# The RG-LRU gates computed per block of 88 instead of per tile of 128, in five groups between the xr and yr products

## The chip, the cores and the metric

One core of one Trainium2 chip runs the whole program. The metric is the device time of one execution in microseconds. The kernel before takes 2645.93 us, the median of three runs (2645.75 to 2646.18).

## What is computed

Two layers of a streaming encoder trunk on x of shape 1 x 512 x 1024, float32. Each layer is half a SwiGLU feed-forward, a mixing block, and another half feed-forward. The change lies in the mixing block's branch A:

```python
def block_diag_linear(x, w, b):                       # 16 blocks of 88 channels
    xb = x.reshape(B, S, RNN_BLOCKS, RNN_BLOCK_DIM)
    return jnp.einsum('bshi,hij->bshj', xb, w).reshape(B, S, D_RNN) + b

def rg_lru(x, w_a, b_a, w_x, b_x, lam):               # D_RNN = 1408 = 16 * 88 = 11 * 128
    r = jax.nn.sigmoid(block_diag_linear(x, w_a, b_a))
    i = jax.nn.sigmoid(block_diag_linear(x, w_x, b_x))
    log_a = -LRU_C * r * jax.nn.softplus(-lam)
    inp = jnp.sqrt(-jnp.expm1(2.0 * log_a)) * (i * x)
    # h[s] = exp(log_a[s]) * h[s-1] + inp[s], a scan over the 512 positions
    ...

xr, yr, q, k, v, g_a, g_b = split(h @ w_in)
u = causal_depthwise_conv(xr)                         # width 4
y_a = (gelu(yr) * rg_lru(u)) @ w_up_a
y_b = chunked_attention(q, k, v) @ w_up_b
x = x + (sigmoid(g_a) * y_a + sigmoid(g_b) * y_b) @ w_out
```

## The kernel before

Everything is held feature-major: a tile is 128 features by 512 positions, and a product leaves one tile in one PSUM bank. Each float32 value is split into a high part and a low remainder, and each product (`product`, L1237 to L1244) is three matmuls: high weight with low activation, high with high, low weight with high activation.

**The ring.** Weights come in chunks of up to 128 x 1024. Each goes through four steps: SP loads it into `raw` (`load`, L341 to L347), ACT copies its high part (`ring`, L511), POOL subtracts to make the low part (L470), and PE uses it. There are four slots. ACT may convert a chunk once PE has begun the third chunk before it; SP may load one once POOL has made the low part of the fourth before it. Each engine's order is written out by hand, so a wait on one engine also delays everything written behind it there. SP has only the loads and the band loads of the attention in its queue.

**Order of the mixing block on PE.** The eleven xr tiles (five `pair` calls of two chunks each and one `single`), then the recurrence gates, then the eleven yr tiles, the eight g_a tiles, w_up_a, q and k, the attention, w_up_b, w_out. One pair is 48 matmuls.

**xr and u.** DVE scales an xr tile out of its bank into `tmp` (L992), which frees the bank. ACT starts the convolution (`conv_init`, L642), DVE adds three taps (`conv`, L1000, `tmp` and `u` in SBUF), ACT takes u's high part (`conv_hi`, L648) and DVE its low part (L839). Two tiles are handled at a time.

**The gates.** The two 1408 x 1408 matrices are block-diagonal with blocks of 88, and the tiles are of 128, so each output tile draws on up to three input tiles. `rg_blocks` lists 52 blocks of weights per layer; 42 are used whole and 10 hold two half-height parts, used by two matmuls on different rows of the array: 186 matmuls (L1389). All come after the last xr product. ACT turns each bank into a gate by a sigmoid (L519), DVE multiplies u by the input gate (L1027). Then ACT runs tanh (L682), and the chain of logarithms and exponentials (L692 to L700) alternates with DVE's subtraction, product and scan (L1041 to L1049). DVE's `yr_out`, which frees the yr banks, stands between its scans. Last come gelu (L712) and the split of the result (`ya_hi`, L524; `ya_lo`, L839), with ring steps of ACT between them.

**Banks.** The products from xr on use six banks in turn (`mix_bank`).

**The attention.** For each of eight pairs of heads, PE turns ten blocks of the probabilities per head by transposes in three groups (`turn`, L1493), with the first two of eight steps of a g_b product between them, computes the next pair's scores (L1435), the other six steps, and the weighted sum (L1508):

```python
turn(0)
gate_b([0])
turn(1)
gate_b([1])
turn(2)
if t + 1 < KD:
    scores(t + 1, (*LATE, 0, 1))
gate_b([2, 3, 4, 5, 6, 7])
weighted(t)
```

All three groups go through the same two banks, 4 and 5.

## Time and profile before

| | us |
|---|---|
| median of three runs | 2645.93 |
| the profiled execution's own time | 2646.78 |
| its span in the trace | 2644.6 |
| PE busy, share of the span | 2636.7, 100% |
| ACT, POOL, DVE busy | 1117.8, 1142.4, 909.0 |
| DMA, share of 16 engines by the queue of SP | 31.8% |

The profile was taken in an execution of its own, 0.85 us above the median of the runs; its span leaves out 2.2 us around the first and last instruction. Matmuls are pipelined: one row lasts 0.39 us although the next starts 0.227 us behind it, so time on PE is read from the starts of successive rows, and not from the durations.

### The profile page before, as it was taken

The page shows a single profiled execution, that of the slowest core. Times are in us where ns is not written, and L with a number is a line of the kernel's source. Part 1 is how long each engine was busy: PE and PEld are TensorE (multiplying, and loading weights), DVE is VectorE, ACT ScalarE, POOL GpSimd, SP SyncE. Part 2 cuts the span into 40 slices and gives each one's busy share as a digit, 9 for nine tenths or more (in the row PEclk, how much of TensorE's full clock was granted, in tenths as well). Part 3 has the DMA queues.
Part 4 walks back from the last instruction along what each step waited for, and adds up shares of the span by engine and source line. Part 5 has one row for each costly group of instructions (what it writes and reads, how often), then busy time and mean ns, then how long its engine had stood idle before and what let it go on. Part 6 is the DMA issues. An engine that isn't in the chain of part 4 may idle for free.

```text
span 2644.6 us, 32094 instructions
## 1 busy us (share of the span) xinstructions
PE 2636.7 (100%) x11988; PEld 2141.2 (81%) x11988; DVE 909.0 (34%) x1585; ACT 1117.8 (42%) x1621; POOL 1142.4 (43%) x484
## 2 busy tenths in 40 slices
PE   9999999999999999999999999999999999999999
PEld 7888887888876788888888888878888768888887
DVE  4223137651345332221132231567313453322210
ACT  5333235742546443332243332457435464433321
POOL 4444444445431344444444444444553313444443
PEclk9999999999999999999999999999999999999999
DMA  5333633333322323332333333332333232333322
GB/s 160 96 95 100 223 92 87 98 93 110 91 72 88 97 81 110 95 95 96 97 103 95 95 93 98 95 92 81 102 106 99 64 105 88 90 101 95 95 92 76
DMA packets 255233, 260.64 MB, mean 99 GB/s; under 512 B 9056, under 2 KB 241536, under 8 KB 255136
## 3 DMA queue, kind: packets, MB, share of 16 engines
q1 hardware_dynamic: 250640, 250.71, 31.8%
q10 hardware_dynamic: 4496, 8.57, 1.0%
q8 instruction: 68, 1.11, 0.2%
q14 instruction: 29, 0.24, 0.0%
HBM read 257.07 MB, written 10.57 MB: 101 GB/s over the span
## 4 chain that ended last, share of the span: by engine, by line
PE 97%; DVE 1%; ACT 1%; DMA 0%; issue 0%; SPq 0%; POOL 0%; DVEq 0%; ACTq 0%; POOLq 0%
PE ps L1239 29%; PE ps L1244 29%; PE ps L1243 29%; PE ps L1389 2%; PE ps L1493 1%; PE ps L1435 1%; PE ps L1508 1%; PE ps L1453 1%; PE ps L1458 1%; PE ps L1457 1%; DVE u L1000 1%; PE ps L1416 0%; PE ps L1415 0%; ACT p L779 0%; DMA raw<-in_w_in 0%
## 5 line engine op out<-in xcount | busy, mean ns | idle before, releaser
L470 POOL TENSOR_TENSOR wlo<-raw,whi 128x1024 fp32r<-128x1024 f32 x472 | 1141.0, 2421 | 1480.8 <-ACT whi L511 1480.8
L1239 PE MATMUL ps<-h_lo,whi 128*128 128x512 f32 x2272 | 889.2, 391 | 0.1
L1244 PE MATMUL ps<-h_hi,wlo 128*128 128x512 f32 x2272 | 884.5, 389 | 0.0
L1243 PE MATMUL ps<-h_hi,whi 128*128 128x512 f32 x2272 | 884.1, 389 | 0.0
L511 ACT ACTIVATE whi<-raw 128x1024 fp32r<-128x1024 f32 x472 | 495.2, 1053 | 708.9 <-PE ps L1239 670.2
L1239 PEld LDWEIGHTS ps<-h_lo,whi 128*128 128x128 f32 x2272 | 426.5, 188 | 93.2 <-issue 4.6
L1244 PEld LDWEIGHTS ps<-h_hi,wlo 128*128 128x128 f32 x2272 | 426.4, 188 | 89.3
L1243 PEld LDWEIGHTS ps<-h_hi,whi 128*128 128x128 f32 x2272 | 426.6, 188 | 86.5
L1239 PE MATMUL ps<-act_lo,whi 128*128 128x512 f32 x704 | 274.0, 389 | 0.0
L1244 PE MATMUL ps<-act_hi,wlo 128*128 128x512 f32 x704 | 273.9, 389 | 0.0
L1243 PE MATMUL ps<-act_hi,whi 128*128 128x512 f32 x704 | 273.9, 389 | 0.0
L889 DVE TENSOR_TENSOR tmp<-ps,square 128x512 f32<-128x512 f32 x88 | 60.9, 691 | 387.4 <-PE ps L1244 387.4
L524 ACT ACTIVATE act_hi<-tmp 128x512 f32 x88 | 55.0, 633 | 240.5 <-DVE tmp L894 240.5
L1244 PEld LDWEIGHTS ps<-act_hi,wlo 128*128 128x128 f32 x704 | 132.1, 188 | 27.7
L1243 PEld LDWEIGHTS ps<-act_hi,whi 128*128 128x128 f32 x704 | 132.1, 188 | 27.3
L1239 PEld LDWEIGHTS ps<-act_lo,whi 128*128 128x128 f32 x704 | 132.1, 188 | 27.2
L905 DVE SCALAR_TENSOR_TENSOR x<-ps,x 128x512 f32<-128x512 f32 x32 | 22.0, 688 | 384.2 <-PE ps L1244 384.2
L884 DVE TENSOR_TENSOR gate<-ps,square 128x512 f32<-128x512 f32 x88 | 60.5, 691 | 263.5 <-PE ps L1244 252.9
L573 ACT ACTIVATE gate<-gate 128x512 f32<-128x512 f32 x88 | 55.2, 631 | 110.1 <-DVE gate L884 110.0
L779 ACT ACTIVATE p<-p,mx 128x512 f32<-128x512 f32 (+3 forms) x128 | 70.1, 550 | 23.1 <-DVE mx L1137 23.1
L1000 DVE SCALAR_TENSOR_TENSOR u<-tmp,par,u 128x511 f32<-128x511 f32 (+2 forms) x66 | 75.4, 1155 | 4.3 <-ACT u L642 2.8
L894 DVE TENSOR_TENSOR tmp<-tmp,gate 128x512 f32<-128x512 f32 x88 | 70.2, 839 | 0.0
(173 smaller groups left out, 2656.3 us busy)
## 6 DMA issues: line engine op xcount, KB each, us to landing
raw<-in_w_in SPq DMA_DIRECT2D x124, 512.0 KB, 3.8
raw<-in_w_gate SPq DMA_DIRECT2D x88, 512.0 KB, 3.8
raw<-in_w_up SPq DMA_DIRECT2D x88, 512.0 KB, 3.8
raw<-in_w_down SPq DMA_DIRECT2D x80, 512.0 KB, 3.5
rel_band<-rel_rows ACTq DMA_DIRECT2D x1, 8192.0 KB, 41.8
raw<-in_w_up_b SPq DMA_DIRECT2D x16, 512.0 KB, 4.0
raw<-in_w_out SPq DMA_DIRECT2D x16, 512.0 KB, 3.5
raw<-in_rg_band SPq DMA_DIRECT2D x14, 448.0 KB, 3.4
```

Of the source, the lines that this page charges most:

```text
L470: nc.gpsimd.tensor_tensor(wlo[:, s, :], raw[:, s, :], whi[:, s, :].bitcast(F32), ALU.subtract).then_inc(lo_made, 1)
L511: nc.scalar.activation(whi[:, s, :], raw[:, s, :], ACT.Copy).then_inc(hi_made, C.made(hi_made))
L524: nc.scalar.activation(dst, src, ACT.Copy).then_inc(split_hi, C.made(split_hi))
L573: nc.scalar.activation(gate[:, m, :], gate[:, m, :], ACT.Silu).then_inc(silu_made, C.made(silu_made))
L779: nc.scalar.activation(part, part, ACT.Exp, scale=-1.0, bias=mx[:, e, i:i + 1], accum_out=total[:, e, i:i + 1]).then_inc(exp_made, C.made( ...
L884: nc.vector.tensor_tensor(gate[:, m, :], ps[:, m, :], rstd, ALU.mult).then_inc(bank_read[m], C.made(bank_read[m]))
L889: nc.vector.tensor_tensor(tmp[:, m, :], ps[:, 2 + m, :], rstd, ALU.mult).then_inc(bank_read[2 + m], C.made(bank_read[2 + m]))
L894: nc.vector.tensor_tensor(tmp[:, m, :], tmp[:, m, :], gate[:, m, :], ALU.mult).then_inc(to_split, C.made(to_split))
L1000: ins = nc.vector.scalar_tensor_tensor(u[:, t, back:S], tmp[:, t % 2, 0:S - back], col("conv_w", (CONV - 1 - back) * KR + t), u[:, t, back ...
L1239: ins = pe.matmul(ps[:, b, :], w_hi, x_lo, start=start, stop=False)
L1243: pe.matmul(ps[:, b, :], w_hi, x_hi, start=False, stop=False)
L1244: return pe.matmul(ps[:, b, :], w_lo, x_hi, start=False, stop=stop)
```

## The change

The gates are computed per block of 88. One block is six matmuls of 88 rows and 88 columns, 96 per layer. For that u's two parts must lie block by block from partition 0, and the gates must come back tile by tile. Both ways go by DMA from SBUF to SBUF, issued by SP, between its loads. A block crosses a tile's edge or not, so it is one or two pieces: 26 pieces for 16 blocks. Each piece is one DMA for u (both parts), one for the gate r and one for the gate i. Three buffers take blocks of u, two take blocks of gates.

The order on PE becomes: xr tiles 0 to 5, blocks 0 to 2, xr 6 and 7, blocks 3 to 5, xr 8 and 9, blocks 6 to 8, xr 10, blocks 9 and 10, yr 0 and 1, blocks 11 to 15, yr 2 to 10. The gates' weights are five chunks in place of eight. The xr tile is now scaled in its bank and stays there until the convolution has read it.

```diff
+NB = RNN // RB
+GROUPS = [(0, 3), (3, 6), (6, 9), (9, 11), (11, 16)]
+HELD = 3
@@ SP
+            def u_moves(l, b):
+                sp.wait_ge(u_split, l * KR + pieces(b)[-1][0] + 1)
+                if b >= HELD:
+                    sp.wait_ge(for_act, KD + l * 2 * NB + 2 * (b - HELD + 1))
+                for m, p0_, p1_, to in pieces(b):
+                    sp.dma_start(block_u[b % HELD][to:to + p1_ - p0_, :, :].bitcast(F32),
+                                 u_parts[p0_:p1_, :, m, :].bitcast(F32)).then_inc(u_moved[b % HELD], 16)
+            def gates_move(l, b):
+                sp.wait_ge(gate_made, l * 2 * NB + 2 * b + 1)
+                for m, p0_, p1_, to in pieces(b):
+                    sp.dma_start(r[p0_:p1_, m, :], block_gates[b % 2][to:to + p1_ - p0_, 0, :]
+                                 ).then_inc(gates_moved[b % 2], 16)
+                sp.wait_ge(gate_made, l * 2 * NB + 2 * b + 2)
+                for m, p0_, p1_, to in pieces(b):
+                    if m >= HELD:
+                        sp.wait_ge(gated, l * KR + m - HELD + 1)
+                    sp.dma_start(i_gate[p0_:p1_, m % HELD, :], block_gates[b % 2][to:to + p1_ - p0_, 1, :]
+                                 ).then_inc(gates_moved[b % 2], 16)
...
+                half_pair(YR0, 3, 1)
+                gates_move(l, 11)
+                u_moves(l, 14)
+                gates_move(l, 12)
+                u_moves(l, 15)
+                gates_move(l, 13)
+                half_pair(YR0, 4, 0)
+                gates_move(l, 14)
+                gates_move(l, 15)
+                half_pair(YR0, 4, 1)
@@ ACT
+                def gates(first, last):
+                    for b in range(first, last):
+                        if l or b >= 2:
+                            act.wait_ge(gates_moved[b % 2], moved(l, b, 2, 2) - 32 * len(pieces(b)))
+                        for g in range(2):
+                            act.wait_ge(for_act, C.next(for_act))
+                            nc.scalar.activation(block_gates[b % 2][0:RB, g, :], ps[0:RB, BANK["gate", 2 * b + g], :],
+                                                 ACT.Sigmoid, bias=col("b_x" if g else "b_a", b)[0:RB, :]
+                                                 ).then_inc(gate_made, C.made(gate_made))
...
+                decayed(6, 7)
+                ring()
+                gates(11, NB)
+                ring()
+                decayed(7, KR)
@@ DVE
+                def xr_out(b):
+                    dve.wait_ge(for_dve, C.next(for_dve))
+                    nc.vector.tensor_tensor(ps[:, b, :], ps[:, b, :], rstd_mix[:, :], ALU.mult
+                                            ).then_inc(xr_scaled, C.made(xr_scaled))
@@ DVE, conv
-                            u[:, t, back:S], tmp[:, t % 2, 0:S - back], col("conv_w", (CONV - 1 - back) * KR + t),
+                            u[:, t, back:S], ps[:, b, 0:S - back], col("conv_w", (CONV - 1 - back) * KR + t),
@@ DVE
+                u_made(8, 9)
+                u_gated(4, 5)
+                u_made(10)
+                u_gated(6)
+                yr_out(0)
+                yr_out(1)
+                u_gated(7, 8, 9, 10)
@@ PE
+                def gates(first, last):
+                    s = chunk()
+                    for b in range(first, last):
+                        pe.wait_ge(u_moved[b % HELD], moved(l, b, HELD, 1))
+                        for g in range(2):
+                            to, at = BANK["gate", 2 * b + g], (2 * (b - first) + g) * RB
+                            bank_free(to)
...
@@ PE, attention
                     turn(0)
-                    gate_b([0])
                     turn(1)
-                    gate_b([1])
                     turn(2)
                     if t + 1 < KD:
-                        scores(t + 1, (*LATE, 0, 1))
-                    gate_b([2, 3, 4, 5, 6, 7])
+                        scores(t + 1, (2, 0, 3, 1))
+                    gate_b(list(range(KD)))
                     weighted(t)
```

`moved` gives the count that a semaphore has once a block's pieces have landed. `bank_free` waits for the bank's last reader, for a gate's bank also for its sigmoid. With banks given out in PE's new order, the last two gates of each of the first three groups fall on the banks of the two xr tiles just before them (`BANK`). In the attention, the second group of transposes goes through banks 1 and 3 (`TURN_BANK`), the others stay in 4 and 5. The sigmoid's table of ACT is loaded ahead of the first convolution, and tanh is spread between the groups (`decayed`). `yr_out` of tiles 0 and 1 comes ahead of the scans, the others move back accordingly. The loops of POOL over the ring are written anew, with the same instruction per chunk. The gates' biases are laid out per block, ten columns more in `par`.

## Rows read from the trace of the kernel before

**Rows 1.** The page: its heading, busy time, the chain by engine.
```profile
span 2644.6 us, 32094 instructions
PE 2636.7 (100%) x11988; PEld 2141.2 (81%) x11988; DVE 909.0 (34%) x1585; ACT 1117.8 (42%) x1621; POOL 1142.4 (43%) x484
PE 97%; DVE 1%; ACT 1%; DMA 0%; issue 0%; SPq 0%; POOL 0%; DVEq 0%; ACTq 0%; POOLq 0%
```

**Rows 2.** Timeline of PE, gates of layer 0: start, length, engine, line, operation.
```profile
433.29 0.39 PE L1389 MATMUL ps<-u_lo,whi 128*128 128x512 f32 x1
...
444.57 0.47 PE L1389 MATMUL ps<-u_lo,whi 128*128 128x512 f32 x1 [0.73 <-ACT r L519]
...
473.96 0.39 PE L1239 MATMUL ps<-h_lo,whi 128*128 128x512 f32 x1
...
478.72 0.39 PE L1239 MATMUL ps<-h_lo,whi 128*128 128x512 f32 x1
```

**Rows 3.** Timeline of PE, first gate and first yr matmul of layer 1.
```profile
1745.33 0.39 PE L1389 MATMUL ps<-u_lo,whi 128*128 128x512 f32 x1
...
1786.02 0.39 PE L1239 MATMUL ps<-h_lo,whi 128*128 128x512 f32 x1
```

**Rows 4.** Timeline of DVE: second tile scaled, then the six taps of xr 4 and 5.
```profile
406.29 0.69 DVE L992 TENSOR_TENSOR tmp<-ps,rstd_mix 128x512 f32<-128x512 f32 x1 [0.20 <-PE ps L1244]
406.98 7.58 DVE L1000 SCALAR_TENSOR_TENSOR u<-tmp,par,u 128x511 f32<-128x511 f32 x6
```

**Rows 5.** Two lines of DVE over the run: shortest, median, longest in ns.
```profile
L1000 DVE SCALAR_TENSOR_TENSOR u<-tmp,par,u x66: 737/750/2896, 386.9 to 1752.1; 128x511 f32<-128x511 f32 x22, 128x510 f32<-128x510 f32 x22, 128x509 f32<-128x509 f32 x22
...
L905 DVE SCALAR_TENSOR_TENSOR x<-ps,x x32: 679/691/692, 281.5 to 2640.2; 128x512 f32<-128x512 f32 x32
```

**Rows 6.** Timeline of POOL beside those taps.
```profile
408.87 2.92 POOL L470 TENSOR_TENSOR wlo<-raw,whi 128x1024 fp32r<-128x1024 f32 x1 [0.67 <-ACT whi L511]
```

**Rows 7.** Timeline of ACT: a sigmoid, a ring step, first logarithm, first ya_hi.
```profile
444.32 0.68 ACT L519 ACTIVATE gate<-ps,par 128x512 f32<-128x512 f32 x1
444.89 1.06 ACT L511 ACTIVATE whi<-raw 128x1024 fp32r<-128x1024 f32 x1
...
485.01 0.63 ACT L697 ACTIVATE gate<-scan 128x512 f32<-128x512 f32 x1
...
533.75 0.63 ACT L524 ACTIVATE ya_hi<-tmp 128x512 fp32r<-128x512 f32 x1 [6.94 <-DVE tmp L1056]
```

**Rows 8.** SP's issues: back to back at L412 (ns), their landing; a weight load's landing.
```profile
L412 SPq DMA_DIRECT2D tmp<-rel_band x44: 444/597/599, 692.0 to 2165.7; - x44
...
DMA to landing us min/median/max: 2.3/2.7/4.7
...
raw<-in_w_in SPq DMA_DIRECT2D x124, 512.0 KB, 3.8
```

**Rows 9.** Stages: busy us per engine, granted clock, DMA share, GB/s.
```profile
0.00:5.00 5.00, 2.81 (x13) 2.81 (x14) 0.00 (x0) 1.28 (x1) 1.30 (x12) 1.00 0.53 166
5.00:10.00 5.00, 4.73 (x35) 4.33 (x34) 0.00 (x0) 1.34 (x2) 2.35 (x1) 1.00 1.01 322
400.00:480.00 80.00, 79.27 (x361) 60.24 (x360) 51.20 (x53) 45.20 (x61) 35.60 (x16) 1.00 0.33 93
```

**Rows 10.** Timeline of PE through one pair of heads.
```profile
791.38 1.09 PE L1493 MATMUL ps<-ident,p 128*128 128x128 f32 x8
792.23 0.47 PE L1239 MATMUL ps<-h_lo,whi 128*128 128x512 f32 x1
...
795.15 2.43 PE L1435 MATMUL ps<-k,q 64*128 64x512 f32 x16
797.51 0.50 PE L1239 MATMUL ps<-h_lo,whi 128*128 128x512 f32 x1
...
804.13 1.09 PE L1493 MATMUL ps<-ident,p 128*128 128x128 f32 x8
```

**Rows 11.** Timeline of ACT, the second copy out of the transposes' banks.
```profile
792.57 0.59 ACT L792 ACTIVATE square<-ps 128x512 f32<-128x512 f32 x1
```

More of the change, by code:

```diff
@@ L338, in _, with load @@
             place = [0]
-            def load(src, shape):
+            def load(src, shape, held=P):
                 s = place[0] % SLOTS
@@ new lines, in gate_weights, with half_pair, last_tile @@
+                def gate_weights(n):
+                    first, last = (2 * b * RB for b in GROUPS[n])
+                    load(bands[:, bass.ds(l, 1), first:last], (1, last - first), RB)
+                def half_pair(base, j, g):
+                    a, b = G8[g]
+                    load(win[:, bass.ds(l * KD + a, b - a), base + j * PAIR:base + (j + 1) * PAIR], (b - a, PAIR))
+                def last_tile(base):
+                    load(win[:, bass.ds(l * KD, KD), base + (KR - 1) * P:base + KR * P], (KD, P))
@@ L663, in _ @@
-                conv_init(KR - 1)
-                conv_hi(KR - 1)
-                chunks = 0
-                for m in range(KR):
-                    for g in range(2):
-                        while chunks * BPC <= rg_at(m, g)[-1]:
-                            ring()
-                            chunks += 1
-                        if g and m >= 2:
-                            act.wait_ge(gated, C.next(gated))
-                        read(mix_bank(RG_T + 2 * m + g), gate[:, m % 2, :] if g else r[:, m, :], ACT.Sigmoid,
-                             bias=col("b_x" if g else "b_a", m))
@@ new lines, in decayed @@
+                def decayed(first, last):
+                    for m in range(first, last):
+                        act.wait_ge(gated, C.next(gated))
+                        nc.scalar.activation(scan[:, m, :], r[:, m, :], ACT.Tanh, scale=decay[:, 0, m:m + 1]
+                                             ).then_inc(tanh_made, C.made(tanh_made))
+                sum_high()
+                ring(2)
+                rstd_from(0, rstd_mix[:, :])
+                act.preload_act_table_set("sigmoid_and_others")
@@ new lines, in _ @@
+                C.step(bank_read[1])
+                conv_init(0)
+                conv_init(1)
+                ring()
+                conv_hi(0)
+                conv_hi(1)
+                ring()
+                conv_init(2)
+                conv_init(3)
+                ring()
+                conv_hi(2)
+                conv_hi(3)
+                ring()
+                conv_init(4)
+                conv_init(5)
+                ring()
+                gates(0, 3)
+                conv_hi(4)
@@ L1016, in _, with yr_out, ga_out, u_made @@
+                def yr_out(t):
+                    scaled(y[:, t, :], BANK["yr", t])
+                def ga_out(t):
+                    scaled(ya_out[:, t, :], BANK["g", t])
+                def u_made(*tiles):
+                    for t in tiles:
+                        xr_out(BANK["xr", t])
+                    dve.wait_ge(xr_scaled, C.now(xr_scaled))
+                    if tiles[0] == 2:
                         dve.wait_ge(col_turned, C.next(col_turned))
                         nc.vector.tensor_copy(rstd_col[:, :], ps[:, 1, 0:S:P]).then_inc(bank_read[1], C.made(bank_read[1]))
-                    for n in both:
-                        conv(n)
@@ L1020, in _ @@
-                    for n in both:
-                        lo_of(u_lo[:, n, :], u[:, n, :], u_hi[:, n, :])
-                for m in range(KR):
-                    C.step(bank_read[mix_bank(RG_T + 2 * m)])
-                    C.step(bank_read[mix_bank(RG_T + 2 * m + 1)])
-                    dve.wait_ge(bank_read[mix_bank(RG_T + 2 * m + 1)], C.now(bank_read[mix_bank(RG_T + 2 * m + 1)]))
-                    nc.vector.tensor_tensor(u[:, m, :], u[:, m, :], gate[:, m % 2, :], ALU.mult
-                                            ).then_inc(gated, C.made(gated))
```

387 lines of the change are left out of this document (210 added, 177 removed).

## The prediction

> **What bounds the kernel now.** I read the page first: PE is busy for the whole span, and the chain that ended last is 97% PE [rows 1]; the granted clock is 1.00 in the stages that I read [rows 9]. So only two things change the time: how many matmul slots PE is given, and how long it waits between them. Then the timeline of PE around the gates: the first gate matmul starts at 433.29, the first yr matmul at 473.96, so the gates hold PE for 40.67 us, with one wait of 0.73 us inside [rows 2]. In layer 1 it is 1745.33 to 1786.02, 40.69 us [rows 3]. There is no hidden idle to win back; what is to win is the slots themselves. The timelines of DVE, ACT and POOL and the issues of SP then give the lengths of the links that the new hand-over is made of.
>
> **Part 1, fewer matmuls.** 186 matmuls, of which 60 go two at a time, are 156 slots. Plain matmuls follow each other at 0.2267 us: 21 of them lie from 473.96 to 478.72 [rows 2], so the 48 of a pair of tiles take 10.88. 16 blocks x 2 gates x 3 are 96 matmuls. The stream is 512 positions long as before, whatever the 88 rows and columns, so I keep 0.2267: 21.76 us. No row has an 88-row matmul; the nearest ones, of 128 rows, set the price, and half-height ones came in at 40.67 / 156 = 0.26 per slot with their changes of form, which do not recur here. The layer saves 40.68 - 21.75 = 18.9 us, both layers **-37.8**.
>
> **Part 2, the attention.** From the first transposes (791.38) to the scores (795.15) are 3.77 us, with six product matmuls in them [rows 10]. Eight transposes take 0.85 (791.38 to 792.23), so twenty take 2.13; the six products then cost 6 x 0.2267 = 1.36 at the end of the turn. 3.77 - 2.13 - 1.36 is 0.28 for the changes of form that go. The third group needs bank 4 and 5 copied out: the second copy ends at 793.16 [rows 11], and its transposes would reach bank 5 at about 791.38 + 1.7 + 0.2 = 793.3, so no wait, though by a hair. The scores move from 3.8 to 2.1 us into the turn, so softmax gets time rather than losing it. I take 0.25 x 16 turns = **-4.0**, bounds 0 and -4.5.
>
> **Part 3, banks held by the convolution.** An xr tile used to leave its bank with the scaling. Now it stays until its last tap. In groups one to three the last two gates want the banks of the two xr tiles just finished. Take group one: the xr pair ends near 406.0, the second scaling runs 406.29 to 406.98, then come six taps [rows 4]. Those took 7.58 us, since one tap sat through POOL's subtraction (up to 2.90 us for one) [rows 5, 6]. The tap now reads PSUM, like the update of x at L905, which in 32 instances never passed 0.692 us [rows 5]. So six taps at 0.76 (start to start, each waits for the one before) are 4.6: the bank is free at 411.5. PE starts the last gate at 411.7 and ends at 412.4, where without waits it would end at 406.0 + 18 x 0.2267 = 410.1. That is 2.3 us, three times per layer: **+13.8**. Bounds: 0.4 us less if a PSUM tap is at 0.69, 2.4 more if POOL still holds it.
>
> **Part 4, the round trips.** 26 pieces x 3 are 78 DMAs per layer in SP's queue. Back to back an issue takes 0.60 us [rows 8], so they hold SP for some 47 us of the 80 in question. Landing: the band loads of at most 128 KB took 2.7 us in the median, a 512 KB load 3.8 [rows 8]; for 176 KB of gate I take 2.8, for 352 KB of u 3.4. They ride on more traffic than before: 5.8 MB of u and 5.8 of gates per layer on top of 93 GB/s come to about 230 GB/s [rows 9], but 322 has been moved at full share [rows 9].
>
> I walked the queues with these links, a sigmoid at 0.6 and a ring step at 1.06 [rows 7]. Groups one, two and four find their u in time. Two places don't hold:
> - u_gated(4, 5) stands on DVE before u_made(10) and waits for block 8's gates to be back. Block 8's sigmoid itself waits for block 6's to leave its buffer. That is some 2 us after xr 10 is finished, and then come scaling, start and three taps; yr 1 wants that bank 2.7 us after yr 0 began. PE waits 1.3 us: **+2.6** for two layers.
> - Group five, from its start at 0: ring step to 1.3, the two sigmoids of block 11 to 2.5, its four gate DMAs from 1.9 to 4.3, and only then SP sends u of block 14 (two issues, the second at 4.9), which lands at 8.3. PE wants it at 18 x 0.2267 = 4.1. Then block 12's two DMAs, u of block 15 sent at 6.1 to 6.7, landed near 10. PE ends at 11.3 instead of 6.8: **+9.0** for two layers. If issues and landings are hidden better it is 0; one more us of landing adds one.
>
> What is covered: the loads written behind these moves. The worst, the load of yr 8's first chunk, is issued some 8 us late into group five, while ACT wants it over 20 us later. DVE has room: it was busy 51 of 80 us, and loses the held taps [rows 9]. ACT's sigmoids, tanh and the table load only move. POOL's loops are free, since POOL waits for ACT at each chunk.
>
> **The sum.** -37.8 - 4.0 + 13.8 + 2.6 + 9.0 = -16.4 us. The profiled execution's 2646.78 would become 2630.4, the median of 2645.93 would become **2629.5**. A measurement of this kernel tells about 0.2%, 5.3 us, from no change.
>
> How a DMA is spread is not shown by any row. The Trainium skill (DMA: Bandwidth & Descriptors, Why a DMA increments its semaphore by 16 and not by 1) says that a DMA uses the largest number of engines, up to 16, that divides its slowest dimension: 11 for 88 rows, 8 to 16 for the pieces. By that an estimate for u is some 0.5 us more of landing, which speaks against the change and would make the sum about 4 us smaller. No run here shows it yet.
>
> **The rivals.**
> - *The trips are hidden* (0.22). SP issues at 0.37 with gaps and the sigmoids run early, so group five loses 2 us and yr 1 nothing: -41.8 + 13.8 + 4 = -24, 2622. Against it: a single SP queue in strict order.
> - *The scan chain comes late* (0.17). The logarithms began at 485.0, ya_hi 48.7 us later [rows 7]; the ring step after it gives a chunk 6 us later still, at start + 54.7. With the new order that chunk is due 12 chunks (65.3 us) after group five. By the walk the logarithms begin 7.6 us after group five, so the margin is 3 us. Beyond it each us costs PE one per layer; 3 us late beyond the margin gives 2636.
> - *Landings grow, and the new path becomes the bound* (0.12; ends slower). The place is the chain block 6, block 8, xr 10, and group five. One us more of landing costs about 3 us on yr 1's bank (two trips and one of u) and 1 in group five, 8 for both layers. Above 5.3 us (2 more than I took) the gain is gone; at 6.5 it is 2655. For it: 230 GB/s instead of 93, and band loads that took up to 4.7 us [rows 8]. Against it: the median of those is 2.7.
> - *The clock falls* (0.02). New waits of 1 to 5 us stand where there was one of 0.73 [rows 2]. The row from 0 to 5 us shows a granted clock of 1.00 with PE busy 2.81 [rows 9]. If the clock fell to its lower level, 1.2 instead of 2.4 GHz, for the 96 gate products of each layer, that would be 21.8 more each, 2673. The Trainium skill (TensorE: Matmul & The Clock Gate, Part 1) says that the clock drops when PE has been idle; by that rule it could happen here, the trace so far shows none.
>
> **How the numbers follow.** 0.45 for the forecast (2624 to 2637), 0.22 hidden, 0.17 late chain, 0.12 landings, 0.04 for the clock and the rest. Above 2640.6 lie the landings, the clock and some of the late chain; between 2640.6 and 2651.2 falls half of these. Faster 0.78, same 0.11, slower 0.11. The range 2612 to 2648 holds the forecast, the hidden case and, at its upper end, most of the late chain and the edge of the landings; about 0.15 is outside.
>
> **What would show it.** From the first xr matmul to the first yr 2 matmul, PE's starts give the gates' 96 slots at 0.2267 (right) or wider. Waits of PE for DVE's taps of 0.7 and 1.6 us, in groups one to three. A wait of about 4 us for u's DMA within group five. Waits of PE for POOL's low parts or DVE's yr_out after group five would speak for the late chain. Landings of u's moves over 5 us, or SP never idle between 400 and 480, would make the prediction wrong towards slower; no wait in group five, towards faster.

## The result: 0.5% slower, and the profile after

| | us |
|---|---|
| before, median of five runs (2645.75 to 2647.41) | 2646.18 |
| after, median of five runs (2656.34 to 2661.41) | 2659.47 |
| ratio after to before, 95% interval | 1.0047 (1.0036 to 1.0058) |
| span of the profiled execution after | 2657.7 |

The kernel became 13.3 us slower, where 16.4 us less were forecast. That is outside the range, and on the other side of no change.

The page of after, to be held against [rows 1]: heading, busy time, the granted clock in 40 slices, the chain by engine.

```profile
span 2657.7 us, 32153 instructions
PE 2621.7 (99%) x11808; PEld 2126.4 (80%) x11808; DVE 890.6 (34%) x1585; ACT 1117.8 (42%) x1635; POOL 1128.5 (42%) x478
PEclk9999998899999999999999999998999999999999
PE 95%; DMA 2%; DVE 1%; SPq 1%; ACT 0%; issue 0%; POOL 0%; ACTq 0%; DVEq 0%; POOLq 0%
```

PE has 180 matmuls less, is 15 us less busy, and ends 13.1 us later. The chain has 2% DMA where it had 0%. The clock row dips to 8 in two places, and they are the two mixing blocks.

What PE waited for over the run: line, releaser, total us, times, longest.

```profile
PE ps L1511 <- DMA last_block<-u_parts: 12.9, 4, 6.9
PE ps L1511 <- issue: 6.1, 6, 1.9
PE ps L1511 <- DVE u L1108: 3.2, 4, 1.2
PE ps L1361 <- DVE u L1108: 2.7, 1, 2.7
PE ps L1511 <- DMA square_lo<-u_parts: 2.6, 4, 0.9
...
PE ps L1511 <- DMA square_hi<-u_parts: 2.2, 2, 1.3
```

L1511 is a gate's first matmul. The first row can be blocks 2, 5, 8, 11 and 14, whose u lies in `last_block`; 12.2 of its 12.9 us are block 14, once per layer, the rest block 5 and block 8. "issue" before a gate is a wait that the profile couldn't tie to a releaser; it stands before the first block of a group (0, 3, 6 or 9). The kernel without u's trip, below, has no such row.

Stages of after, to be held against [rows 9]: busy us by engine, granted clock, DMA share, GB/s.

```profile
420.00:430.00 10.00, 10.00 (x45) 7.56 (x43) 5.24 (x7) 4.99 (x7) 3.36 (x3) 1.00 0.90 220
...
480.00:485.00 5.00, 1.59 (x7) 0.77 (x5) 0.69 (x1) 2.24 (x4) 1.23 (x1) 1.00 0.66 191
485.00:490.00 5.00, 2.86 (x6) 1.44 (x6) 0.00 (x0) 0.90 (x3) 0.00 (x0) 0.53 0.64 183
490.00:495.00 5.00, 3.85 (x9) 2.74 (x10) 0.69 (x1) 2.17 (x4) 0.00 (x0) 0.50 0.84 227
400.00:500.00 100.00, 85.08 (x317) 62.09 (x316) 43.24 (x52) 50.22 (x72) 34.53 (x15) 0.86 0.68 182
```

In group five PE is busy 1.59 us of five, and then has the lower clock: granted 0.53 and 0.50, which is 1.2 instead of 2.4 GHz. Over 100 us PE is busy 85 and the granted clock is 0.86.

The matmuls behind the wait, in the timeline of PE (in brackets the idle time and its releaser):

```profile
486.95 0.73 PE L1511 MATMUL ps<-last_block,whi 88*88 88x512 f32 x1 [5.36 <-DMA last_block<-u_parts]
487.47 0.63 PE L1515 MATMUL ps<-last_block,whi 88*88 88x512 f32 x1
487.90 0.63 PE L1516 MATMUL ps<-last_block,wlo 88*88 88x512 f32 x1
...
491.15 0.73 PE L1511 MATMUL ps<-square_hi,whi 88*88 88x512 f32 x1 [1.34 <-DMA square_hi<-u_parts]
```

Starts are 0.43 us apart and not 0.227. So a wait can cost twice: its own length, and the slow slots behind it. Not every wait does: in layer 1 those before blocks 0 and 1 (0.29 and 0.56 us idle) left the clock up.

From PE's starts in each layer, against a slot of 0.2267 us, the 13.1 us come out (each wait is counted from start to start, less a slot, so it is some 0.2 us more than the idle time in the table of waits):

| term, both layers | predicted | measured |
|---|---|---|
| matmul slots | -37.8 | -37.8 |
| attention | -4.0 | -1.5 |
| waits inside and around the gates (16.5 and 17.5 us; 12.7 per layer were predicted) | +25.4 | +34.0 |
| slots at the lower clock (54 and 30, each 0.20 us longer) | 0 | +17.3 |
| restarts and rounding | 0 | +1 to 2 |
| sum | -16.4 | +13 to 14 |

The 34.0 us of waits divide otherwise than predicted: DVE's taps 3.9 (13.8 predicted), u's moves in groups one to four 11.6 (nothing), the bank of yr 1 2.9, all in layer 0 (2.6), blocks 14 and 15 15.5 (9.0).

### The profile page after: what moved, and what is told of

Same layout as the page of the kernel before. It is cut to its first block, busy times and chain, and to the rows that moved or that the text cites. A ratio compares the mean times of both kernels' runs of the same rounds, so it can differ in the third digit from the quotient of the medians.

```text
span 2657.7 us, 32153 instructions
## 1 busy us (share of the span) xinstructions
PE 2621.7 (99%) x11808; PEld 2126.4 (80%) x11808; DVE 890.6 (34%) x1585; ACT 1117.8 (42%) x1635; POOL 1128.5 (42%) x478
## 4 chain that ended last, share of the span: by engine, by line
PE 95%; DMA 2%; DVE 1%; SPq 1%; ACT 0%; issue 0%; POOL 0%; ACTq 0%; DVEq 0%; POOLq 0%
PE ps L1361 29%; PE ps L1365 29%; PE ps L1366 29%; PE ps L1569 1%; PE ps L1627 1%; PE ps L1642 1%; PE ps L1587 1%; PE ps L1592 1%; PE ps L1591 1%; DMA square_lo<-u_parts 1%; DVE u L1108 1%; DMA square_hi<-u_parts 0%; PE ps L1511 0%; SPq L410 0%; SPq L404 0%
## 5 line engine op out<-in xcount | busy, mean ns | idle before, releaser
L563 POOL TENSOR_TENSOR wlo<-raw,whi 128x1024 fp32r<-128x1024 f32 x466 | 1127.2, 2422 | 1507.7 <-ACT whi L587 1507.5
L587 ACT ACTIVATE whi<-raw 128x1024 fp32r<-128x1024 f32 x466 | 489.3, 1054 | 737.8 <-PE ps L1361 700.1
L881 ACT ACTIVATE p<-p,mx 128x384 f32<-128x384 f32 (+3 forms) x128 | 69.9, 548 | 17.9 <-DVE mx L1258 17.9
L1361 PE MATMUL ps<-ya_lo,whi 128*128 128x512 f32 x176 | 68.5, 389 | 0.0
```

The lines of the kernel that those rows point to most:

```text
L563: nc.gpsimd.tensor_tensor(wlo[:, s, :], raw[:, s, :], whi[:, s, :].bitcast(F32), ALU.subtract).then_inc(lo_made, 1)
L587: nc.scalar.activation(whi[:, s, :], raw[:, s, :], ACT.Copy).then_inc(hi_made, C.made(hi_made))
L881: nc.scalar.activation(part, part, ACT.Exp, scale=-1.0, bias=mx[:, e, i:i + 1], accum_out=total[:, e, i:i + 1]).then_inc(exp_made, C.made( ...
L1361: ins = pe.matmul(ps[:, b, :], w_hi, x_lo, start=start, stop=False)
```

## The experiments

Twelve kernels ran, each timed beside the kernel before on the same chip (its medians there: 2646.1 to 2646.6). Ratios are to the kernel before. Single waits are read from the one execution of each kernel that was profiled.

### Without u's trip

```diff
-                u_moves(l, 0)
...
-                        pe.wait_ge(u_moved[b % HELD], moved(l, b, HELD, 1))
+                        m_ = pieces(b)[0][0]
+                        pe.wait_ge(u_split, l * KR + pieces(b)[-1][0] + 1)
...
-                            u_b = block_u[b % HELD]
+                            u_b = u_parts[:, :, m_, :]
```

> The changed kernel without the DMAs of u: PE reads the two parts of u's tile where they lie, partitions 0 to 87 of the tile in which the block begins, so the gates see the wrong channels of u; the products, the gates' way back and every other order stay. Theory A (the round trip of u makes the long waits, and the lower clock follows from them): the waits of 5.5 and 7.0 us before block 14 and those before blocks 0, 1, 6 and 15 go, only the taps' bank waits of 0.5 to 1.4 us and what the gates' way back makes remain, some 7 us per layer; the lower clock (11.0 and 6.3 us in the two layers) goes as well. 2659.5 - 34.0 + 14 - 17.3 = about 2622 us. Theory B (the gates' way back and SP's queue make them): waits in group five stay near 7 us, time above 2640. Theory C (the lower clock comes from the 88-row matmuls themselves, not from waits): slots of 0.43 us stay, about 2640.

Measured: 2636.9 us, ratio 0.9966 (0.9952 to 0.998). The waits for u's DMA are gone and the lower clock nearly so (7 slots at it per layer instead of 54 and 30). It is 22.6 us below after, but 15 above the expectation of 2622. The waits of PE account for some 10 of the 15, the slots left at the lower clock for 3:

```profile
PE ps L1496 <- DVE u L1092: 10.1, 12, 1.2
PE ps L1345 <- POOL wlo L547: 8.7, 6, 2.5
```

The first row is the banks held by the taps, as forecast. The second is new: the late scan chain, one of the rivals. The first logarithm starts at 489.26, 14.4 us behind the last gate product, where after had 8.0. With u's trip away PE is through group five in 6.9 us instead of 16.5, while the first logarithm still comes 21.3 us behind the group's start (24.6 in after).

### Work in place of idle time

```diff
+                def fill(n):
+                    for _ in range(n):
+                        pe.matmul(ps[:, 0, :], h_hi[:, 0, 0:P], h_hi[:, 0, :], start=True, stop=True)
...
+                        fill(({0: 6, 1: 4, 6: 6, 14: 23, 15: 5}, {0: 1, 1: 3, 6: 4, 7: 3, 9: 8, 10: 4, 14: 29, 15: 4})[l].get(b, 0))
                         pe.wait_ge(u_moved[b % HELD], moved(l, b, HELD, 1))
```

> The changed kernel with matmuls that nobody reads, on bank 0, put on PE ahead of its waits for u, sized to each layer's waits (44 in layer 0, 56 in layer 1). Nothing is left out. Theory A (the clock falls because PE waits): the granted clock stays at 1.00 through the gates, and 11.0 + 6.3 = 17 us come back; the waits' length in all stays, now filled. About 2643 us. Theory C (the clock falls for the form of the gates' matmuls): no gain, 2660 or above.

Measured: 2653.52 us, ratio 1.0029 (1.0018 to 1.0041). The same group five as above:

```profile
480.00:485.00 5.00, 4.73 (x21) 3.57 (x19) 0.69 (x1) 0.85 (x2) 0.00 (x0) 1.00 0.79 203
485.00:490.00 5.00, 2.88 (x12) 1.87 (x13) 0.00 (x0) 1.67 (x3) 0.00 (x0) 1.00 0.65 188
```

The clock stays at 1.00 here with the same 88-row matmuls and 100 filler products of no use. So it is the idle time, and not the form of the products, that lowers it. Over both layers about 17 slots are left at the lower clock instead of 84, so some 14 of the 17 us came back. Only 6 show in the time, which ranged from 2650.5 to 2658.2: in the profiled execution waits and fillers together take 37.7 us instead of 34.0, since the fillers do not fit the waits exactly, and PE comes to the first gate 2 us later than in after.

### The attention alone

Before, with only the attention's part of the change.

```diff
-        TURN_BANK, OUT_BANK, GB_BANK = (4, 5), 6, 7
+        TURN_BANK, OUT_BANK, GB_BANK = ((4, 5), (1, 3), (4, 5)), 6, 7
...
-                    gate_b([0])
...
-                    gate_b([1])
...
-                        scores(t + 1, (*LATE, 0, 1))
-                    gate_b([2, 3, 4, 5, 6, 7])
+                        scores(t + 1, (2, 0, 3, 1))
+                    gate_b(list(range(KD)))
```

> The kernel before with only the attention's part of the change: banks 1 and 3 for the second group of transposes, scores in the order 2, 0, 3, 1, the whole g_b product behind them. In the changed kernel one turn took 12.66 us in place of 12.75. If that is its whole worth: -1.5 us, 2644.7. By my prediction's term it would be -4.0, 2642.2. If the order had hidden costs elsewhere: 0 or above.

Measured: 2644.44 us, ratio 0.9993 (0.9983 to 1.0002). The interval just holds 1, though all ten times lie below all of the kernel before. PE's timeline in this run:

```profile
791.29 2.40 PE L1495 MATMUL ps<-ident,p 128*128 128x128 f32 x20
793.63 2.43 PE L1437 MATMUL ps<-k,q 64*128 64x384 f32 x16
```

Twenty transposes take 2.32 us in the median up to the scores, where I had scaled 2.13 from eight. In the last pair, where a product follows them, they take 2.15. So the scaling was right, and it is the change from transposes to scores that costs 0.17 us; it was there before the change too (four transposes 0.585 us up to the scores, 0.411 up to a product), and I had counted it among those that go.

### u's moves on ACT's queue

```diff
-                sp.wait_ge(u_split, l * KR + pieces(b)[-1][0] + 1)
+                act.wait_ge(u_split, l * KR + pieces(b)[-1][0] + 1)
...
-                gates(11, NB)
+                gates(11, 12)
+                u_moves(l, 14)
```

> The changed kernel with u's DMAs issued by ACT in place of SP; the u moves of blocks 14 and 15 stand right behind the sigmoids of blocks 11 and 12. The gates' way back and the loads stay with SP. Nothing is left out. If SP's single queue makes the late start of u (four gate DMAs of 0.75 us ahead of u of block 14), the wait before block 14 falls by about 3 us in each layer, the early ones by 1 to 2, and some of the lower clock with them: about 2645 us. If the landing itself is what is slow (5 to 7 us with DMA share above 0.9), the waits fall by 1 us or less and ACT's 26 issues of some 0.85 us delay sigmoids and ring: 2655 to 2665.

Measured: 2668.86 us, ratio 1.0086 (1.0069 to 1.0103): worse than after. Block 14's wait fell from 5.5 and 7.0 to 3.5 and 2.1 us, so the place in SP's queue did cost 2 to 5 us there. But DVE's taps came later (waits of PE for taps 12.7 us, up to 4.0). DVE's product with the input gate stands ahead of the scaling of xr 8, and it waited for the gates' way back; first of after, then of this kernel:

```profile
439.79 1.38 DVE L1143 TENSOR_TENSOR u<-u,i_gate 128x512 f32<-128x512 f32 x1 [1.43 <-DMA i_gate<-square]
```

```profile
446.35 0.69 DVE L1148 TENSOR_TENSOR u<-u,i_gate 128x512 f32<-128x512 f32 x1 [8.30 <-DMA i_gate<-square]
```

SP began to issue these gates at 436.83 in after and at 438.16 here, where ACT sent u's moves at the same time; they came 3.0 and 8.2 us behind that. The Trainium skill (DMA: Bandwidth & Descriptors, Issuing engines are not separate DMA queues) says that all issuers share the same 16 DMA engines; the run agrees, since what the one queue gained the other lost, and u's own landing didn't shorten (the two pieces of block 14 took 6.0 and 4.7 us from the first issue until PE ran on, 4.5 and 6.0 in after).

### 96 rows instead of 88

```diff
+                    if p1_ - p0_ == RB and p0_ + 96 <= P:
+                        p1_ = p0_ + 96
```

> The changed kernel with 96 rows moved in place of 88 for the five blocks that lie in one tile and have the rows to spare (0, 3, 6, 9, 12); the surplus rows land where nothing reads them. Nothing is left out. If the number of DMA engines that share a transfer sets the landing (96 divides by 16, 88 only by 11), u of block 0 lands over 1 us sooner, the waits before blocks 0, 6 and 9 (1.6 and 0.5, 1.6 and 1.0, 0 and 2.0 us) fall by about 1 us each: 2650 to 2655. If the load on the engines as a whole or the path from SBUF sets it: within 3 us of 2659.5. Blocks 14 and 15, with the longest waits, keep their form either way.

Measured: 2656.35 us, ratio 1.0037 (1.0023 to 1.0051), some 3 us below after, with the intervals overlapping. In layer 0 the waits before block 0 and block 6 went from 1.6 to 0.7 and from 1.6 to 1.0 us, but block 3, which had not waited, waited 1.0; in layer 1 those before blocks 0, 3, 6 and 9 (0.5, 0.4, 1.0 and 2.0) went. So the sign of the Trainium skill's rule in my prediction (DMA: Bandwidth & Descriptors, Why a DMA increments its semaphore by 16 and not by 1) agrees with most of these waits. The time doesn't show it: yr 1 waited 6.1 us over both layers instead of 2.7, and block 14, whose pieces the edit doesn't touch, still waited 5.5 and 5.7. A small share of the loss at most.

### Half of u's bytes

```diff
-                    sp.dma_start(block_u[b % HELD][to:to + p1_ - p0_, :, :].bitcast(F32),
-                                 u_parts[p0_:p1_, :, m, :].bitcast(F32)).then_inc(u_moved[b % HELD], 16)
+                    sp.dma_start(block_u[b % HELD][to:to + p1_ - p0_, 0, :].bitcast(F32),
+                                 u_parts[p0_:p1_, 0, m, :].bitcast(F32)).then_inc(u_moved[b % HELD], 16)
...
-                            ins = pe.matmul(ps[0:RB, to, :], w_hi, u_b[0:RB, 1, :], start=True, stop=False)
+                            ins = pe.matmul(ps[0:RB, to, :], w_hi, u_b[0:RB, 0, :], start=True, stop=False)
```

> The changed kernel with only the high part of u moved, 2 KB per row in place of 4; PE uses it for the low part too, so the gates' low product is another one. Same number of DMAs, same queue, half the bytes of u. Theory A (bytes on busy DMA engines make the landing): u lands in 3 to 4 us in place of 5 to 7; the waits before blocks 14 and 15 fall from 7.3 and 8.3 us per layer to 4 to 5, the early ones nearly go, the lower clock falls by half: 2640 to 2645. Theory B (SP's issues, 78 of 0.75 us per layer, and their order make the waits): under 5 us gained, 2655.

Measured: 2649.92 us, ratio 1.0015 (1.0005 to 1.0025), 9.5 below after and between the two expectations. The early waits for u went, block 14's fell to 3.95 us in both layers. The waits for taps came back in their place (9.9 us of idle time, 3.2 in after), and yr 1 waited about 3 us in both layers. The move of block 15's u, in the chain of waits, from the start of its issue to PE; first of after, then of this kernel:

```profile
485.91 5.20 DMA square_hi<-u_parts
```

```profile
480.15 3.52 DMA square_hi<-u_parts
```

352 KB take 5.20 us and 176 KB 3.52. In layer 1 the same moves take 6.16 and 3.65.

### Without u's trip, with ring steps earlier

The first of these kernels, with ACT's ring steps moved ahead within the logarithms and exponentials.

```diff
-                    if m % 2 and m <= KR:
+                    if m in (1, 3, 5, 6, 8, 9):
                         ring()
...
-                    if t in (1, 3, 5, 7, 9, 11):
-                        ring()
+                    if t in (1, 5, 7, 9, 11):
+                        ring(2 if t == 1 else 1)
```

> The kernel of the first of these runs (no DMAs of u, PE reads u's tile in place) with three of ACT's ring steps moved ahead: in the chain of logarithms after m = 6, 8 and 9 in place of 7, 9 and 11, and two behind the second gelu in place of one there and one behind the fourth. If PE's six waits for POOL's low parts (8.7 us) come from where the ring steps stand behind the scan chain, they go: 2636.9 - 8.7 = 2628. If POOL or the loads are what is late: no change. What is left then over the 2606.6 of the matmuls counted out (2646.1 - 37.8 - 1.7) should be the taps' bank waits, 2 x 7.2 us, and 2 to 3 us of lower clock and restarts per layer.

Measured: 2634.33 us, ratio 0.9954 (0.9938 to 0.9971). The waits for POOL fell from 8.7 to 1.1 us, and this came in their place:

```profile
PE ps L1345 <- DVE y L1085: 5.3, 2, 2.9
```

yr's banks now wait for DVE's `yr_out`, which stands between the scans. The place of the ring steps was worth 2.6 us, not 8.7: the chain itself is late.

### A last group of one block

The groups (9, 12), (12, 15), (15, 16) in place of (9, 11), (11, 16), the last one inside yr 2; u's moves ahead of the gates' in SP's queue; the ring steps of the kernel above; DVE starts u_made(10) ahead of u_gated(5). The gates' weights are six chunks here.

```diff
-GROUPS = [(0, 3), (3, 6), (6, 9), (9, 11), (11, 16)]
+GROUPS = [(0, 3), (3, 6), (6, 9), (9, 12), (12, 15), (15, 16)]
...
-                yr(2)
+                yr(2, behind=lambda g: g == 0 and gates(*GROUPS[5]))
```

> The changed kernel with other groups: blocks 9 to 11 behind xr 10, 12 to 14 behind yr 0 and 1, block 15 between the two chunks of yr 2 and 3; u's DMAs ahead of the gates' in SP's queue; xr 10's taps ahead of u_gated(5); the ring steps moved as in the run beside this. Nothing is left out. No block's u now waits for a sigmoid of its own group, so by theory A the waits before blocks 14 and 15 (7.3, 8.3 us) go, and with them most of the lower clock (17.3 us in both layers); the first groups keep theirs, some 9 us per layer: 2659.5 - 15.6 - 12 = about 2632, with late ring steps giving back up to 5. If the landings are so slow that u is late in every order: above 2645.

Measured: 2665.5 us, ratio 1.0075 (1.0058 to 1.0091), a clear miss of 2632. The wait before block 14 went; block 15 still waited 2.1 us in layer 0, block 11 now 4.0 and 2.9, and then:

```profile
PE ps L1374 <- DVE y L1106: 14.7, 5, 6.0
PE ps L1524 <- DMA last_block<-u_parts: 8.0, 5, 3.8
```

The first logarithm starts at 502.65, 14.4 us behind the last gate product, as without u's trip. The order that took the wait from block 14 moved it to the chain behind the gates. The run changes four things at once and doesn't tell which of them did that.

### Without the gates' trip, and without both

```diff
-                gates_move(l, 0)
...
-                            nc.scalar.activation(block_gates[b % 2][0:RB, g, :], ps[0:RB, BANK["gate", 2 * b + g], :],
+                            nc.scalar.activation(i_gate[:, m_ % HELD, :] if g else r[:, m_, :], ps[:, BANK["gate", 2 * b + g], :],
...
-                            dve.wait_ge(gates_moved[b % 2], moved(l, b, 2, 2))
+                        dve.wait_ge(gate_made, l * 2 * NB + 2 * covering(m)[1] + 2)
```

The second of the two kernels has this edit and that of the first experiment.

> The gates' 52 DMAs per layer are gone: each sigmoid writes a tile of r or i_gate in place (128 rows, so the gates lie in the wrong channels and some tiles hold only one block's), DVE waits for the sigmoids. u's 26 DMAs per layer stay. Theory A (u's landing of 5 to 7 us is partly the gates' share of the same DMA engines, and partly its place behind them in SP's queue): u lands in about 4 us, the waits before blocks 0 to 10 for DMA nearly vanish, yr 1's wait goes, block 14 still waits 3 to 4 us since its buffer comes free only with block 11's sigmoids; lower-clock loss about 7 us per layer; 2646.4 - 39.5 + 11 of bank waits + 8 at block 14 + 14 of clock + 2 = 2642 (2638 to 2647). Rival B (u's landing is its own size on its own engines, the gates' traffic beside it costs nothing): landings stay at 5 to 7 us, block 14 waits 5 us or more, and the time stays above 2650.

> Both trips gone: u read in place and the gates written in place, both in the wrong channels, so all that is left of the change is the fewer matmuls, the new order with its bank waits, and the attention. Theory A (the late chain of the kernel without u's trip, 8.7 us of waits for POOL's low parts after group five, comes from the gates' trip back, which holds the last tanh and so the logarithms): logarithms begin 2 to 3 us sooner, the waits for POOL drop to 2 us or less, 2646.4 - 39.5 + 11 of bank waits + 2 to 4 = 2620 to 2623. Rival B (the chain is late by the order itself: five blocks behind yr 0 and 1, and ring steps at fixed places between the exponentials): the waits for POOL stay near 6 to 9 us and the time is 2627 to 2634.

Measured: without the gates' trip 2630.05 us, ratio 0.994 (0.9927 to 0.9954), 29.4 below after, better than either theory had it; its five times lie between 2629.24 and 2635.76, and the profiled execution took 2635.02. Without both 2621.73 us, ratio 0.991 (0.9895 to 0.9925), in the expected 2620 to 2623.

The move of block 15's u in the chain of waits: without the gates' trip in both layers, then in layer 1 of after (layer 0 is above, 5.20). The last row is the stage around the first of them.

```profile
475.49 5.21 DMA square_hi<-u_parts
...
1778.86 5.13 DMA square_hi<-u_parts
```

```profile
1801.29 6.16 DMA square_hi<-u_parts
```

```profile
475.00:481.00 6.00, 3.45 (x14) 1.85 (x13) 3.14 (x3) 3.63 (x6) 1.20 (x1) 1.00 0.78 196
```

The landing of 4 us that theory A expected didn't come: 5.2 and 5.1 us, against 5.2 and 6.2 in after. From its second issue until PE ran on, block 14's u took 3.2 us in both layers, against 3.8 and 5.3. So the gates' traffic cost u nothing to 2 us, and rival B was right on most of the landing, though not on the time. The DMA engines' share doesn't tell the difference: 0.78 while the move was under way here, 0.63 and 0.74 in the two layers of after. Most of the gain lies elsewhere. Group five of both kernels shows where: SP's issues and ACT's sigmoids of after, then those without the gates' trip.

```profile
477.70 1.06 ACT L587 ACTIVATE whi<-raw 128x1024 fp32r<-128x1024 f32 x1 [0.62 <-PE ps L1511]
478.67 1.24 ACT L727 ACTIVATE square<-ps,par 88x512 f32<-88x512 f32 x2
...
479.36 1.51 SPq L404 DMA_DIRECT2D r<-square  x2
480.97 1.37 SPq L410 DMA_DIRECT2D i_gate<-square  x2
482.45 1.55 SPq L397 DMA_DIRECT2D last_block<-u_parts  x2
...
483.81 1.26 ACT L727 ACTIVATE square<-ps,par 88x512 f32<-88x512 f32 x2 [2.76 <-DMA i_gate<-square]
```

```profile
472.67 1.06 ACT L571 ACTIVATE whi<-raw 128x1024 fp32r<-128x1024 f32 x1 [3.77 <-PE ps L1495]
473.63 0.67 ACT L714 ACTIVATE r<-ps,par 128x512 f32<-128x512 f32 x1
...
473.88 1.51 SPq L397 DMA_DIRECT2D last_block<-u_parts  x2
```

Group five begins at 477.27 and at 472.24. In after u of block 14 is sent 5.2 us behind that, behind 3.0 us of gate issues; without the gates' trip it is sent after 1.6. And ACT no longer stands 2.76 us until block 11's gates have left their buffer. The waits for block 14 are 1.3 us per layer, those of yr's first matmul for DVE are gone, and so is most of the lower clock (31 and 7 slots).

Without both trips the first logarithm starts 5.6 us behind the last gate product and PE waits for none of POOL's low parts: the late chain of the first kernel was the gates' way back. What is left of PE's waits:

```profile
PE ps L1480 <- DVE u L1079: 10.1, 12, 1.2
```

### Fewer issues, and u first

In the first of the last two kernels the two gates of a piece go back by one DMA; in the second u's moves also stand ahead of the gates' in groups four and five.

```diff
-                sp.wait_ge(gate_made, l * 2 * NB + 2 * b + 1)
-                for m, p0_, p1_, to in pieces(b):
-                    sp.dma_start(r[p0_:p1_, m, :], block_gates[b % 2][to:to + p1_ - p0_, 0, :]
-                                 ).then_inc(gates_moved[b % 2], 16)
...
-                    sp.dma_start(i_gate[p0_:p1_, m % HELD, :], block_gates[b % 2][to:to + p1_ - p0_, 1, :]
+                    both = r_i[p0_:p1_, m:KR + m % HELD + 1:KR + m % HELD - m, :]
+                    sp.dma_start(both, block_gates[b % 2][to:to + p1_ - p0_, :, :]
```

```diff
+                u_moves(l, 14)
                 gates_move(l, 11)
-                u_moves(l, 14)
+                u_moves(l, 15)
                 gates_move(l, 12)
-                u_moves(l, 15)
```

> r and i_gate lie in one tensor, and each piece's two gates go back by one DMA with a strided destination: the same bytes, 26 issues per layer instead of 52; the computation is complete. Without the gates' moves the kernel took 2630.1, 29.4 less than after. In group five u of block 14 was then sent 1.6 us after the group's start and landed 2.3 us behind its second issue; in after it was sent 5.2 us after the start, behind 3.0 us of gate issues, and landed 2.95 behind them. Theory A (the place lost in SP's queue is most of it): u of block 14 is sent 1.2 to 1.5 us sooner, the wait before it falls by as much in both layers, waits before blocks 0 to 13 shrink too, the lower-clock loss shrinks with them: 2646 to 2653. Rival B (the gates' bytes on the DMA engines, and the two-way trip that sigmoids and DVE wait for): nothing of this changes, within 3 us of 2659.5.

> The same, and in groups four and five u's move of a block stands in SP's queue ahead of the gates' move that it followed (u 14 ahead of gates 11, u 15 ahead of gates 12, and so for 9, 10, 12, 13). Theory A: u of block 14 is sent 2 us after the group's start and PE waits for it 1.5 to 2.5 us instead of 5.5 and 7.0; gates come back some 1.6 us later there, which the last sigmoids and the chain may feel by 1 to 2 us per layer: 2640 to 2648, at or below the kernel before. Rival B (what the gates lose, u gains, so that the chain and yr_out's banks come late, as they did with the groups of three): not below v2_one_gate_dma by more than 2 us, with waits of PE for POOL's low parts or DVE's y behind group five.

Measured: 2667.33 us, ratio 1.008 (1.0067 to 1.0094), and 2664.87 us, ratio 1.0065 (1.0051 to 1.0079). Both are slower than after. The first kernel's issues and sigmoids in group one:

```profile
409.89 0.89 SPq L408 DMA_DIRECT2D r_i<-tmp  x1
...
415.10 1.26 ACT L725 ACTIVATE tmp<-ps,par 88x512 f32<-88x512 f32 x2 [4.09 <-DMA r_i<-tmp]
```

One move of 352 KB takes 5.2 us here too, from its issue to the sigmoid that waits for the buffer. In after, with two moves of 176 KB, ACT had no wait for the DMA at this place, but there PE was later too. The kernel without u's trip has the two moves with PE as early as here:

```profile
412.96 1.26 ACT L711 ACTIVATE tmp<-ps,par 88x512 f32<-88x512 f32 x2 [2.50 <-DMA i_gate<-tmp]
```

There ACT stood 2.50 us instead of 4.09, and the second of the two moves took 3.2 us from its issue. In the kernel with one move block 2's gates, then the ring step and the next u are late, and PE waits 3.7 and 2.8 us before block 3. Half the issues were worth less than what the longer move cost, together with a second price of the edit: r now waits for the second sigmoid and, as i_gate does, for a free tile of i_gate.

Sending u first cut block 14's wait from 4.8 and 7.1 to 1.65 and 1.59 us, as expected. It gave 3.9 of these 8.6 us back before yr 1, which wants the bank of xr 10: 4.7 and 4.4 us instead of 2.9 and 2.3. Blocks 10 and 15 wait 3.3 us more in all, and there are 2.0 us of waits for POOL behind group five. The time is 2.5 us below the first of the two, with the intervals overlapping: nearer to rival B, what u gains there the gates lose.

## Why the prediction was wrong, step by step

- **Part 1, slots: right.** At the full clock the 88-row products start 0.227 us apart, and 37.8 us are saved.
- **Part 2, attention: right in sign, too large.** 1.5 to 1.7 us instead of 4.0. I took 0.28 us per turn for changes of form that go. The change from the last transposes to the scores, 0.17 us, is one of them in my sum and stays.
- **Part 3, banks held by the taps: right as a mechanism, but not a term to be added.** Six taps took 4.54 us (4.6 forecast), below what they took in [rows 4], and in the kernel without trips the waits are 0.6 and 1.4 us per group, 2.0 together where 2.3 was forecast. In after itself they come to 3.9 us and not 13.8, since PE stands for u before them in most groups.

```profile
407.12 4.54 DVE L1108 SCALAR_TENSOR_TENSOR u<-ps,par,u 128x511 f32<-128x511 f32 x6
```

- **Part 4, the round trips: this step failed.** I had summed 11.6 us for them and called the u of groups one, two and four in time. In after the waits for u alone are 27 us: 15.5 before blocks 14 and 15, where 9.0 was forecast, and 11.6 before other blocks, where nothing was. Leaving both trips out gives 37.7 us, the lower clock with it. The structure of group five was right: block 14's u behind block 11's gates, PE waiting for both. The sizes were not. An issue took 0.74 to 0.90 us in the median by kind, not the 0.60 of [rows 8], and a block's 352 KB in one piece landed in 5.2 to 7.1 us, not in 3.4. I had drawn a line between band loads of 128 KB and a weight load of 512 KB in [rows 8], which came from another memory. Both errors recur in the other groups: blocks 0 and 1 of layer 0, and 9 and 10 of layer 1, waited 1 to 2 us too. The 2.6 us for yr 1's bank met 2.9, but all in one layer: that agreement is luck.
- **The clock: put at nothing in the sum, the rival at 0.02 took place in part.** I had priced it for all 96 products; 54 and 30 slots ran at 1.2 GHz, 17.3 us. That is more than the whole loss of 13.3. By subtraction after would be at about 2642 without it, 4 us below before, but no run shows this: with the clock held up by fillers the kernel still took 2653.5. The row I held against it, a granted clock of 1.00 with PE busy 2.81 us of the first five in [rows 9], is one stage at the start of the program; it doesn't show what repeated waits do. Here PE busy 2.86 us of five, behind 1.59 of five, had 0.53. The Trainium skill's statement that I cited (TensorE: Matmul & The Clock Gate, Part 1) that idle time drops the clock held; it deserved a chance of its own near that of the forecast's waits.
- **Landings grow:** the rival's mechanism is the one that came, and above 5.3 us of landing I had the gain gone. I gave it 0.12 because of the median of the band loads, the wrong row. I also let waits and clock be separate cases, though the one brings the other.
- **The scan chain late:** not in after, where logarithms began 8.0 and 7.6 us behind the last gate product (7.6 forecast, 3 us of margin). It came in the experiments that mended PE's waits alone. At 14.4 us it cost 4.4 us per layer (without u's trip), and at 11.1 us (u first) 1.0 per layer: the margin of 3 us and one for one beyond it fit these two. They don't fit the kernel with a last group of one block, where at the same 14.4 us PE waited 8 us per layer.

The trips share buffers, ACT's and DVE's orders and SP's queue. Taking away u's gives 22.6 us, the gates' 29.4, both 37.7; the first two add to 52, so much of the waiting goes with either trip. That each lengthens the other through the shared queue and buffers is how I read this; the runs show it in group five only.

**Open.** How the landing divides into a fixed part and bytes while several moves run is not settled: 352 KB in one piece took 5.7 to 7.1 us at the head of a group of three blocks, 5.2 and 6.2 for block 15, and once 9.0 (block 9 of layer 1, where the profile names no releaser). More gate buffers, to end ACT's wait for the way back without longer moves, were not tried. Of the kernels that leave neither trip nor half of u out, none beat the one before by more than the uncertainty; the attention's part alone, without the gates' change (2644.44), comes nearest.

## What to carry to other kernels

Where PE is busy all the time, price a new hand-over by its waits and by the slots at the lower clock behind each: here 34 us of short waits brought 17 us more. Price a copy between places in SBUF from a row of such a copy of the same size, count it as a latency for every engine that waits for its buffer, and follow the whole loop (product, sigmoid, way back, buffer free, next product), not only the first waiter. Mending one wait in such a loop shows the next: measure the kernel with the whole loop cut out first, since it tells what the loop costs.

## What the runs showed of the hardware

- A copy from SBUF to SBUF on 88 partitions in one piece (block 15) took 5.2 and 6.2 us for 352 KB in the two layers of after, and 3.5 and 3.7 for 176 KB, from the start of its issue until PE ran on. Without the gates' traffic 352 KB took 5.2 and 5.1. The profile has no landing of its own for these copies. Where three blocks were sent together, the second piece of block 1, 192 KB behind 512 KB sent just before, took 7.32:

```profile
402.87 7.32 DMA square_lo<-u_parts
```

- The Trainium skill (DMA: Bandwidth & Descriptors, Anatomy of one DMA — SWDGE (gpsimd) path) gives, for GpSimd's path, 2.0 us and bytes at 436 GB/s; by that an estimate for 352 KB is 2.8 us. The two measured sizes differ by 1.7 us in layer 0 and 2.5 in layer 1 for 176 KB; an estimate from these is 70 to 110 GB/s. Here the measurement decides.
- For the engine that waited, two moves of 176 KB in a row were better than one of 352 KB, in spite of the issue saved: ACT stood 2.50 us for the two and 4.09 for the one.
- Idle times of 0.46 and 1.22 us within one group were enough in layer 1 of the kernel without both trips for 7 slots at the lower clock; in layer 0 the same waits left the clock up. The last of these waits and a product behind it, 0.63 us long where it lasts 0.39 at the full clock:

```profile
1710.68 0.47 PE L1480 MATMUL ps<-u_parts,whi 88*88 88x512 f32 x1 [1.22 <-DVE u L1079]
...
1711.61 0.63 PE L1329 MATMUL ps<-h_lo,whi 128*128 128x512 f32 x1
```

- SP took 0.74 to 0.90 us in the median for an issue of these copies, and up to 2.85:

```profile
L397 SPq DMA_DIRECT2D last_block<-u_parts x20: 627/837/2853, 403.6 to 1798.5; - x20
```

- A tap of DVE that reads PSUM took 0.739 to 0.751 us in all 66 instances of after, six in a row 4.54, and was not held up by POOL, where the one with both operands in SBUF took up to 2.9 us [rows 5].
